# Tiles 0 and 1 on shared conv weight pieces, lent ring slots, casts in list order, six sgb buffers

## The chip, the cores and the metric

The kernel runs as one program on the eight cores of one Trainium2 chip; each core works on two of the sixteen sequences, with no exchange between cores. The metric is the device time in microseconds (us) of the slowest core. Engines are PE (TensorE), ACT (ScalarE), DVE (VectorE), POOL (GpSimd) and SP (SyncE); SP and POOL issue DMAs, and only POOL issues those that cast float32 to bfloat16.

## What is computed

One residual block (D_MODEL 1024, RG_W 1280, 16 heads of 80), from the reference:

```python
mod = silu(c) @ w_ada + b_ada; shift, scale, gate = split(mod, 3)
h = rmsnorm(x, g_norm) * (1 + scale) + shift
sc_b, sc_c, sc_v, sc_g, rg_v, rg_g, m_a, m_b = split(h @ w_in)     # 8704 columns
y_a = (sc_b * causal_conv3(sc_c * sc_v) * silu(sc_g)) @ sc_w_out
v = causal_conv4(rg_v)
r = sigmoid(v @ w_a + b_a); i = sigmoid(v @ w_x + b_x)             # block-diagonal
log_a = -8 * r * softplus(-lam)
y_rg[t] = exp(log_a) * y_rg[t-1] + sqrt(1 - exp(2 * log_a)) * i * v
y_b = (y_rg * silu(rg_g)) @ rg_w_out
merged = sigmoid(m_a + b0) * y_a + sigmoid(m_b + b1) * y_b
out = rmsnorm(x + gate * (merged @ w_out), g_final)
```

## The kernel before

A core's 4096 rows are eight tiles of 512 (NT = 8, tiles 0 to 3 are one sequence, 4 to 7 the other). Activations lie transposed, channels on partitions, so a product of 128 output channels is eight matmuls of 128x128 on 128x512 into one of seven PSUM banks. The work is a list of items (`program`, L243), each a letter with a tile and a number:

- P (L455): load 128 rows of x, Square with row sum on ACT, scale into xn (which lies in the four sgb buffers). T (L461): eight transposes of xn, two ACT evictions with scale and shift into hT.
- A, B (L494, L516): one of eight conv pieces, two products each (16 matmuls), output in pa. R (L533): one of ten RG-LRU channel blocks, two products; ACT copies into rbuf and vbuf and takes the tanh for the gate into sgb (L553), DVE does three taps (L555) and frees the gate's bank (L559). R uses vbuf and sgb number n % 4.
- G (L565): the block-diagonal gates of one block, 4 or 6 matmuls in all, from the resident weights wg; tanh and exp on ACT. After each odd block one pair of square roots (L602, L603) with a table load, then `g_tail` (L608) for both: product, scan, product with sgb into prg (L617).
- Z, Y (L619, L631): merge gates (16 matmuls) and the two down projections (8 and 10) of piece M; POOL adds into merged (L658). L, O (L664, L667): x rows again; output projection from resident wout (16 matmuls), gate, residual, norm, store.
- ADA, PRM, GATE (L740, L721, L766): the modulation from c. ADA uses four pieces at the start, GATE two, and writes gatebc, which O needs.

FIRST lists tile 0's A, R, G and tile 1's P, T. Then rounds of MIX: R, G of tile i between Z, Y of tile i - 1, then A, B of tile i between O of tile i - 1 and P, T of tile i + 1. LAST ends tile 7.

Weights stream through a ring of five slots of 1 MB (`ring`, NSLOT). The order of pieces is that of their first use. `pump` (L387) gives the next piece the next free slot: for tile 0 (and ada, gt) a cast DMA on POOL from float32, else a reload on SP from scratch wsc. At its first use a tile-0 piece is also stored to wsc on SP (`get`, L413; the DMA is issued at L418). `used` (L422) frees a slot after the piece's last item and pumps. wg is loaded ahead of piece A1, wout ahead of gt0, both with no wait since their buffers are their own.

The order of instructions on each engine is made by `Sched.schedule` (L97) from durations and dependences. PE keeps the list's order. Each other engine takes, among operations whose predecessors have been placed, the one with the earliest start and, among equals, the lowest index (L129). All engines then run in that order, SP and POOL too: a DMA that has to wait holds all that follow it on its queue.

Of the kernel before, what the change touches and what calls it, by code (L numbers as in the profile page):

```python
# [12 lines left out]
D = 1024  # L13
# [7 lines left out]
NSLOT = 5  # L21
PAD = 16
# [12 lines left out]
class Op:  # L35
    __slots__ = ("idx", "e", "fn", "raw", "order", "dur", "lat", "nbytes", "dsem", "pos", "fin")

    def __init__(self, idx, e, fn, dur, lat, nbytes, dsem):
        self.idx, self.e, self.fn, self.dur, self.lat, self.nbytes, self.dsem = idx, e, fn, dur, lat, nbytes, dsem
        self.raw, self.order = set(), set()  # L40
        self.pos = None
        self.fin = None


class Sched:
# [51 lines left out]
    def schedule(self):  # L97
# [9 lines left out]
        link = 0.0  # L107
# [8 lines left out]
        while done < n:  # L116
            best = None
            for e in ENGS:
# [6 lines left out]
                else:  # L125
# [3 lines left out]
                    cand = min((max(free[e], ready_at[i]), i, e) for i in lst)  # L129
# [87 lines left out]
def gate_pairs():  # L217
    pairs = []
    for j in range(NRC):
# [5 lines left out]
        for i in sorted(ins):  # L225
# [10 lines left out]
FIRST = ("R0 R1 A0 B0 R2 G0 R3 G1 A1 B1 R4 G2 A2 B2 R5 G3 A3 B3 R6 G4 R7 A4 B4 G5 R8 G6 R9 G7 A5 B5 G8 G9 P0 P1 P2 P3 "  # L236
         "A6 B6 T0 A7 T1 B7 T2 T3")
MIX = ("R0 R1 Z0 Y0 R2 Z1 G0 R3 Y1 G1 R4 Z2 G2 Y2 R5 Z3 G3 R6 Y3 G4 Z4 R7 G5 Y4 R8 Z5 G6 Y5 R9 Z6 G7 Y6 G8 Z7 G9 Y7 "
       "A0 B0 P0 P1 P2 L0 A1 B1 P3 L1 O0 A2 B2 L2 O1 A3 B3 L3 O2 A4 T0 B4 O3 A5 T1 B5 A6 T2 B6 A7 T3 B7")
# [3 lines left out]
def program():  # L243
# [4 lines left out]
    for i in range(NT + 1):  # L248
        text = FIRST if i == 0 else MIX if i < NT else LAST
        for word in text.split():  # L250
            k, j = word[0], int(word[1:])
            t = i - 1 if k in "ZYLO" else i + 1 if k in "PT" else i
            if t == NT:
                continue
            if i == 1 and word == "L0":
                p += [("GATE", 0), ("GATE", 1)]
            p.append((k, t, j))
# [3 lines left out]
def piece_of(it):  # L261
# [7 lines left out]
    if k in "AB":  # L269
        return ("A", it[1], it[2])  # L270
# [5 lines left out]
def build_nc():  # L276
# [30 lines left out]
    junk = sb([128, D], BF16, "junk"); junkB = S.buf("junk")  # L307
# [3 lines left out]
    pa = sb([128, 8, TT], BF16, "pa"); paB = [S.buf(f"pa{j}") for j in range(8)]  # L311
# [11 lines left out]
    merged = sb([128, 8, TT], BF16, "merged"); mergedB = [S.buf(f"mg{j}") for j in range(8)]  # L323
    ident = sb([128, 128], BF16, "ident"); identB = S.buf("ident")
    identf = junk[:].bitcast(F32)[:, 0:128]
    ones = junk[:].bitcast(F32)[:, 128:256]
# [49 lines left out]
    ring_state = {"next": 0, "free": list(range(NSLOT)), "where": {}}  # L376
# [10 lines left out]
    def pump():  # L387
        while ring_state["next"] < len(order) and ring_state["free"]:
            key = order[ring_state["next"]]
            slot = ring_state["free"].pop(0)  # L390
# [3 lines left out]
            dst = ring[slot][:, 0:nco]  # L394
            if key[0] in ("ada", "gt") or key[1] == 0:
# [59 lines left out]
    def it_P(i, s):  # L455
        xb, xbB = load_x(i, s)
        assert not any(o[1] < NRC and (o[0], o[1]) in gstate for o in owner.values())
        st, colB = rstd_of(xb[:], [xbB])
        dve(lambda e: e.tensor_scalar(out=xn[:, s, :], in0=xb[:], scalar1=st, scalar2=None, op0=ALU.mult), [xbB, colB], [xnB[s]], 0.75)

    def it_T(i, q):  # L461
# [3 lines left out]
        def tr(e):  # L465
            for kl in range(2):
                kc = 2 * q + kl
                for s in range(4):
                    ins = e.transpose(out=pst[:, kl, s * 128:(s + 1) * 128], in_=xn[:, s, kc * 128:(kc + 1) * 128], identity=ident[:])  # L469
            return ins  # L470
        S.op("pe", tr, reads=xnB + [identB], writes=[pstB], dur=1.0, lat=0.25)
# [22 lines left out]
    def it_A(i, j):  # L494
        key = ("A", i, j)
# [20 lines left out]
    def it_B(i, j):  # L516
        key = ("A", i, j)
# [8 lines left out]
        dve(lambda e: e.tensor_tensor(out=ub[:], in0=bb[:, :], in1=ub[:], op=ALU.mult), [bbB, ubB], [ubB])  # L526
        dve(lambda e: e.tensor_tensor(out=pa[:, j, :], in0=ub[:], in1=gb[:], op=ALU.mult), [ubB, gbB], [paB[j]])
# [5 lines left out]
    def it_R(i, j):  # L533
        key = ("R", i, j // 2)
# [7 lines left out]
        sg_, sgB_ = sgb[:, k, :], sgbB[k]  # L542
# [88 lines left out]
    def it_YM(i, j):  # L631
# [4 lines left out]
        w, wB = get(key)  # L636
        bya, byaB = nb()
# [15 lines left out]
        used(key)  # L653
        dve(lambda e: e.scalar_tensor_tensor(out=ga_[:], in0=ga_[:], scalar=1.0, in1=bya[:, :], op0=ALU.add, op1=ALU.mult),  # L654
# [247 lines left out]
```

How the kernel before makes its waits and increments, by code:

```python
            def body(engine):  # L171
                seen = {}
                def need(tokens):
                    want = {}
                    for sem, val in tokens:
                        if seen.get(sem, 0) < val and want.get(sem, 0) < val:
                            want[sem] = val
                    for sem, val in want.items():
                        seen[sem] = val
                        engine.wait_ge(sched.semobj[sem], val)
                for i in streams[e]:
                    o = ops[i]
                    need([ops[d].pos for d in sorted(o.raw)]
                         + [ops[d].pos for d in sorted(o.order) if e != "pe" or ops[d].e != e])
                    o.fn(engine).then_inc(sched.semobj[o.pos[0]], 16 if o.dsem is not None else 1)
                if e == "sp":
                    need([o.pos for o in last])
```

## Time and profile before

| | us |
|---|---|
| median of 3 runs | 1620.74 |
| lowest, highest | 1616.59, 1670.92 |
| the profiled execution | 1620.76 |
| its span on the slowest core (core 1) | 1619.2 |
| spans of the other cores | 1612.3 to 1618.9 |
| PE, DVE, ACT, POOL busy | 1437.8, 977.4, 882.9, 301.4 |

Busy times are sums over one core's span. Matmul records overlap a little, so a busy PE is not PE at its peak. Times of rows are us from the start of the span, on core 1; the granted clock is 1.00 at 2.4 GHz and 0.50 at 1.2 GHz.

### The profile page before, as it was taken

The numbers are of one execution on the slowest core, as the hardware profiler recorded it, in microseconds if no ns is written. First come the engines' busy times: TensorE is split into PE (matmuls) and PEld (weight loads), VectorE is DVE, ScalarE is ACT, GpSimd is POOL, SyncE is SP. The second block draws the span as 40 slices with busy tenths as digits, with TensorE's granted clock in tenths as the row PEclk, the third lists the DMA queues.
The fourth block names the chain that finished last, engine by engine and source line by source line (L and its number), as shares of the span: only waits on it lengthen the run. The fifth ranks groups of instructions, "written<-read, shape, count | busy, mean of one in ns | idle before, by whom it ended". The sixth has DMA issues, their size and how long they took to land.

```text
span 1619.2 us, 22766 instructions; the slowest of 8 cores (1612.3 to 1619.2 us)
## 1 busy us (share of the span) xinstructions
PE 1437.8 (89%) x6848; PEld 655.1 (40%) x6848; DVE 977.4 (60%) x1435; ACT 882.9 (55%) x1319; POOL 301.4 (19%) x534
## 2 busy tenths in 40 slices
PE   1049829899999999899999999999999999999996
PEld 1024314344444444344444444444444444444442
DVE  2027834577656775568656775568656775567614
ACT  3028835783567645774557645675466735774221
POOL 3002211321112211222111211222112210221011
PEclk9999969999999999999999999999999999999998
DMA  9999985888533563336533464336633474344621
GB/s 183 170 194 207 220 208 129 193 197 270 197 125 119 172 222 138 131 132 207 187 135 109 160 219 148 133 126 204 195 116 132 156 223 148 129 139 143 203 84 65
DMA packets 55688, 265.94 MB, mean 164 GB/s; under 512 B 4880, under 2 KB 6672, under 8 KB 34064
## 3 DMA queue, kind: packets, MB, share of 16 engines
q1 hardware_dynamic: 38592, 231.85, 42.6%
q0 software_dynamic: 16976, 32.64, 13.9%
q8 instruction: 58, 0.95, 0.2%
q14 instruction: 62, 0.51, 0.1%
HBM read 257.78 MB, written 39.32 MB: 183 GB/s over the span
## 4 chain that ended last, share of the span: by engine, by line
PE 83%; DMA 7%; ACT 3%; issue 2%; another core or an unknown queue 2%; DVE 1%; POOL 1%; SPq 0%; ACTq 0%; POOLq 0%; DVEq 0%
PE bank L487 57%; PE bank L650 8%; PE bank L680 7%; PE bank L642 6%; PE bank L582 5%; DMA ring_s<-wall 3%; DMA ring_s<-wm 2%; DMA xb_s<-x 2%; PE pst L469 1%; ACT ab_s L591 1%; DVE sgb_s L559 1%; ACT trb_s L587 1%; ACT gbuf_s L628 1%; ACT sgb_s L553 0%
## 5 line engine op out<-in xcount | busy, mean ns | idle before, releaser
L487 PE MATMUL bank<-hT_s,ring_s 128*128 128x512 bf16 x4352 | 980.8, 384 | 41.5 <-DVE sgb_s L559 37.7
L487 PEld LDWEIGHTS bank<-hT_s,ring_s 128*128 128x128 bf16 x4352 | 427.5, 99 | 565.4 <-issue 72.5
L555 DVE SCALAR_TENSOR_TENSOR vbuf_s<-rbuf_s,cst_s,vbuf_s 128x512 f32<-128x512 f32 x240 | 179.4, 748 | 129.9 <-ACT vbuf_s L551 121.4
L658 POOL TENSOR_TENSOR merged_s<-ubuf_s,gbuf_s 128x512 bf16<-128x512 f32 x64 | 85.7, 1339 | 366.8 <-DVE gbuf_s L656 366.7
L650 PE MATMUL bank<-prg_s,ring_s 128*128 128x512 bf16 x640 | 148.6, 379 | 0.0
L506 ACT ACTIVATE pbuf_s<-bank 128x512 f32<-128x512 f32 x64 | 38.0, 594 | 194.6 <-PE bank L487 177.5
L642 PE MATMUL bank<-pa_s,ring_s 128*128 128x512 bf16 x512 | 120.9, 379 | 0.0
L680 PE MATMUL bank<-wout_s,merged_s 128*128 128x512 bf16 x512 | 116.9, 383 | 2.5 <-POOL merged_s L658 2.5
L550 ACT ACTIVATE rbuf_s<-bank 128x512 f32<-128x512 f32 x80 | 47.5, 593 | 127.3 <-PE bank L487 126.1
L469 PE MATMUL pst<-ident_s,sgb_s 128*128 128x128 bf16 x256 | 21.5, 233 | 105.0 <-ACT hT_s L474 68.4
L596 DVE SCALAR_TENSOR_TENSOR tib_s<-tib_s,vbuf_s 128x512 f32<-128x512 f32 x80 | 61.9, 780 | 72.6 <-ACT tib_s L589 72.6
L582 PE MATMUL bank<-vb_s,wg_s 128*128 128x512 bf16 x416 | 102.7, 379 | 0.0
L616 POOL COPY hst_s<-trb_s 128x1 f32<-128x1 f32 x80 | 78.4, 982 | 121.6 <-DVE trb_s L614 117.0
L614 DVE TENSOR_TENSOR_SCAN trb_s<-ab_s,hst_s,tib_s 128x512 f32<-128x512 f32 x80 | 98.0, 1265 | 0.0
L450 ACT ACTIVATE junk_s<-xb_s 128x1024 bf16<-128x1024 f32 x32 | 33.8, 1056 | 112.2 <-DMA xb_s<-x 106.9
L650 PEld LDWEIGHTS bank<-prg_s,ring_s 128*128 128x128 bf16 x640 | 62.6, 98 | 75.5
L654 DVE SCALAR_TENSOR_TENSOR ubuf_s<-ubuf_s,bank 128x512 f32<-128x512 f32 x64 | 43.7, 683 | 80.9 <-PE bank L642 80.8
L626 ACT ACTIVATE ubuf_s<-bank,prm_s 128x512 f32<-128x512 f32 x64 | 43.9, 686 | 70.0 <-PE bank L487 69.8
L508 DVE TENSOR_TENSOR pbuf_s<-bank,pbuf_s 128x512 f32<-128x512 f32 x64 | 44.1, 689 | 58.7 <-PE bank L487 57.0
L559 DVE SCALAR_TENSOR_TENSOR sgb_s<-sgb_s,bank 128x512 f32<-128x512 f32 x80 | 54.6, 683 | 37.8 <-ACT sgb_s L553 37.6
L680 PEld LDWEIGHTS bank<-wout_s,merged_s 128*128 128x128 bf16 x512 | 50.4, 99 | 64.4 <-issue 5.1
L642 PEld LDWEIGHTS bank<-pa_s,ring_s 128*128 128x128 bf16 x512 | 50.1, 98 | 60.4
(86 smaller groups left out, 1564.9 us busy)
## 6 DMA issues: line engine op xcount, KB each, us to landing
ring_s<-wsc SPq DMA_DIRECT2D x91, 1024.0 KB, 5.7
ring_s<-wsc SPq DMA_DIRECT2D x56, 1088.0 KB, 5.5
xb_s<-x SPq DMA_DIRECT2D x64, 512.0 KB, 5.0
out<-vbuf_s SPq DMA_DIRECT2D x32, 512.0 KB, 4.3
ring_s<-wall POOLq DMA_DIRECT2D x13, 1024.0 KB, 32.9
wsc<-ring_s SPq DMA_DIRECT2D x13, 1024.0 KB, 11.3
ring_s<-wm POOLq DMA_DIRECT2D x8, 1088.0 KB, 13.9
wsc<-ring_s SPq DMA_DIRECT2D x8, 1088.0 KB, 8.9
```

The source lines that it names most:

```text
L487: ins = e.matmul(bk[:, :], lhsT=w[:, o:o + 128], rhs=hT[h][:, kc, :], start=(kc == 0), stop=(kc == 7))
L550: act(lambda e: e.activation(out=rb_[:, 3:3 + TT], in_=brv[:, :], func=AF.Copy), [brvB], [rbB_], 0, True)
L555: dve((lambda e, t=t, w=w: e.scalar_tensor_tensor(out=v_, in0=rb_[:, t:t + TT], scalar=w, in1=v_, op0=ALU.mult, op1=ALU.add)), [rbB_, vB_, ...
L559: dve(lambda e: e.scalar_tensor_tensor(out=sg_, in0=sg_, scalar=1.0, in1=brg[:, :], op0=ALU.add, op1=ALU.mult), [sgB_, brgB], [sgB_])
L582: ins = e.matmul(bk[:, :], lhsT=wg[:, g, gi, :], rhs=rhs_l[t][:], start=(t == 0), stop=(t == len(prs) - 1))
L596: dve(lambda e: e.scalar_tensor_tensor(out=ti_[:], in0=ti_[:], scalar=1.0, in1=v_, op0=ALU.add, op1=ALU.mult), [tiB_, vB_], [tiB_])
L614: dve(lambda e: e.tensor_tensor_scan(out=tr_[:], data0=a_[:], data1=ti_[:], initial=hst[:, j:j + 1], op0=ALU.mult, op1=ALU.add), [aB_, tiB ...
L616: pool(lambda e: e.tensor_copy(out=hst[:, j:j + 1], in_=tr_[:, TT - 1:TT]), [trB_], [hstB[j]])
L642: ins = e.matmul(bya[:, :], lhsT=w[:, o:o + 128], rhs=pa[:, kc, :], start=(kc == 0), stop=(kc == 7))
L650: ins = e.matmul(byb[:, :], lhsT=w[:, o:o + 128], rhs=prg[:, h, kc, :], start=(kc == 0), stop=(kc == NRC - 1))
L658: pool(lambda e: e.tensor_tensor(out=merged[:, j, :], in0=ga_[:], in1=gb_[:], op=ALU.add), [gaB_, gbB_], [mergedB[j]], 1.27)
L680: ins = e.matmul(bk[:, :], lhsT=merged[:, kc, s * 128:(s + 1) * 128], rhs=wout[:, kc, hh * 512:(hh + 1) * 512], start=(kc == 0), stop=(kc ...
```

## The change

1. **Shared A pieces.** `piece_of` gives A and B items of tiles 0 and 1 the same piece, so each conv piece is loaded once for both tiles. R pieces of tile 1 are still reloaded. FIRST and the first MIX become three parts, H0, H1 and H2; lower case r, g, a, b are items of tile 1, V is GATE. Tile 1's conv output goes to `pa_1`, in ring slot 4, which joins the ring after Y7 of tile 1; its xn goes to merged.
2. **Lent slots.** Slots 5 and 6 are the two halves of wout, 7 is gatebc; A pieces 0 to 4 may use 5, 6 and 0 to 3, tile 0's R pieces 7 and 0 to 3, all others 0 to 4.
3. **Late residents.** wg is loaded ahead of R piece 2, wout ahead of M piece 0, waiting for slots 5 and 6.
4. **Scheduler.** Every operation gets a due time: for PE the sum of durations before it, for others that plus SLACK or what its users need. Among equal starts the earlier due goes first. Casts on POOL go in list order. The link's model has its own rate for casts and shares it with SP's transfers. Durations and latencies are set anew.
5. **sgb has six buffers** and R uses n % 6. junk is gone: Square writes its result into xn or the x buffer, and the start's identity and ones lie in vbuf.
6. **Rounds from tile 2 on** are MIXR (the old first half) and MIXA, with T items about one A, B pair earlier.

```diff
@@ schedule
+        t = 0.0
+        for o in ops:
+            if o.e == "pe":
+                o.due = t
+                t += o.dur
+            else:
+                o.due = t + SLACK
+        for o in reversed(ops):
+            for d in o.raw | o.order:
+                p = ops[d]
+                if p.e != "pe":
+                    p.due = min(p.due, o.due - p.dur - p.lat)
...
-                    cand = min((max(free[e], ready_at[i]), i, e) for i in lst)
+                    lst = [i for i in lst if e != "pool" or not ops[i].nbytes or i == casts[cast_next]]
+                    if not lst:
+                        continue
+                    cand = min((max(free[e], ready_at[i]), ops[i].due, e, i) for i in lst)
+                    cand = (cand[0], cand[3], e)
...
+            if o.nbytes and e == "pool":
+                cast_next += 1
+                link["pool"] = max(link["pool"], start + 1.0) + o.nbytes / 292e3
+                o.fin = link["pool"] + o.lat
...
-FIRST = ("R0 R1 A0 B0 R2 G0 R3 G1 A1 B1 R4 G2 A2 B2 R5 G3 A3 B3 R6 G4 R7 A4 B4 G5 R8 G6 R9 G7 A5 B5 G8 G9 P0 P1 P2 P3 "
-         "A6 B6 T0 A7 T1 B7 T2 T3")
...
+H0 = ("A0 B0 R0 R1 P0 P1 P2 P3 A1 B1 T0 R2 T1 G0 T2 R3 T3 G1 a0 b0 R4 G2 a1 b1 R5 G3 A2 B2 R6 G4 a2 b2 R7 G5 A3 B3 R8 G6 a3 b3 R9 G7 "
+      "A4 B4 r0 G8 a4 b4 r1 G9")
+H1 = "A5 B5 r2 g0 a5 b5 r3 g1 V0 A6 B6 r4 g2 a6 b6 r5 g3 V1 A7 B7 r6 g4 a7 b7 r7 g5 Z0 r8 g6 Z1 r9 g7 Y0 g8 Z2 g9"
+H2 = "Y1 P0 Z3 Y2 P1 Z4 Y3 P2 Z5 Y4 P3 Z6 Y5 Z7 Y6 T0 Y7 T1 T2 L0 L1 O0 T3 L2 O1 L3 O2 O3"
+MIXR = ("R0 R1 Z0 Y0 R2 Z1 G0 R3 Y1 G1 R4 Z2 G2 Y2 R5 Z3 G3 R6 Y3 G4 Z4 R7 G5 Y4 R8 Z5 G6 Y5 R9 Z6 G7 Y6 G8 Z7 G9 Y7")
+MIXA = "A0 B0 P0 P1 P2 L0 A1 B1 P3 L1 O0 A2 B2 L2 O1 A3 T0 B3 L3 O2 A4 B4 T1 O3 A5 B5 T2 A6 B6 T3 A7 B7"
...
-        return ("A", it[1], it[2])
+        return ("A", it[1] if it[1] > 1 else 0, it[2])
...
+    pa_1 = ring[NSLOT - 1][:, 0:8 * TT].rearrange("p (k t) -> p k t", k=8); paB_1 = [S.buf(f"pb{j}") for j in range(8)]
...
+    NSG = 6
+    sgb = sb([128, NSG, TT], F32, "sgb"); sgbB = [S.buf(f"sgb{k}") for k in range(NSG)]
...
+    MM = 0.213
+    T_PS = {0: 0.5, 1: 0.59, 2: 0.88}
+    T_SB = {0: 0.53, 1: 0.63, 2: 0.9}
...
+    wflat = wout[:].rearrange("p k n -> p (k n)")
+    slots += [wflat[:, 0:4096], wflat[:, 4096:8192], gatebc[:].rearrange("p b n -> p (b n)").bitcast(BF16)]
...
+    ring_state = {"next": 0, "free": [0, 1, 2, 3, 5, 6, 7], "where": {}}
...
-            slot = ring_state["free"].pop(0)
+            lend = (5, 6, 0, 1, 2, 3) if key[0] == "A" and key[1] == 0 and key[2] < 5 else (7, 0, 1, 2, 3) if key[0:2] == ("R", 0) else range(NSLOT)
+            fit = [k for k in ring_state["free"] if k in lend]
+            if not fit:
+                break
+            slot = min(fit, key=lend.index)
...
-        sg_, sgB_ = sgb[:, k, :], sgbB[k]
+        sg_, sgB_ = sgb[:, n % NSG, :], sgbB[n % NSG]
...
+        if i == 1 and j == 7:
+            ring_state["free"].append(NSLOT - 1)
+            pump()
...
-    before_piece[("A", 0, 1)] = [lambda: S.dma("pool", lambda e: e.dma_start(
+    before_piece[("R", 0, 2)] = [lambda: S.dma("pool", lambda e: e.dma_start(
...
-    before_piece[("gt", 0)] = [lambda: S.dma("pool", lambda e: e.dma_start(out=wout[:], in_=wout_d[:, :, 0:1024]), writes=[woutB],
+    before_piece[("M", 0, 0)] = [lambda: S.dma("pool", lambda e: e.dma_start(out=wout[:], in_=wout_d[:, :, 0:1024]), writes=[woutB] + lentB[0:2],
```

## Rows read from the trace of the kernel before

**Rows 1.** Busy time by stages, core 1; first line: the columns

```profile
core 1: us, PE busy (x) PEld busy (x) DVE busy (x) ACT busy (x) POOL busy (x), PEclk, DMA share, GB/s
0.00:45.00 45.00, 6.84 (x152) 6.15 (x152) 11.85 (x61) 13.96 (x23) 13.35 (x26) 1.00 0.97 181
45.00:100.00 55.00, 0.04 (x1) 0.07 (x2) 0.15 (x1) 1.82 (x3) 0.44 (x1) 1.00 1.07 182
100.00:182.00 82.00, 80.11 (x366) 36.14 (x367) 58.58 (x86) 60.16 (x89) 18.87 (x41) 1.00 1.02 200
182.00:251.00 69.00, 30.77 (x144) 13.59 (x142) 33.54 (x51) 37.50 (x55) 11.49 (x20) 0.72 0.84 208
251.00:439.80 188.80, 184.03 (x869) 83.92 (x870) 123.27 (x174) 109.58 (x164) 40.20 (x70) 0.99 0.77 200
439.80:1530.30 1090.50, 1061.69 (x4986) 482.22 (x4984) 721.61 (x1025) 644.34 (x962) 202.83 (x365) 0.99 0.47 158
```

**Rows 2.** Chain of waits, start-up and first rounds: start us, us, what

```profile
382.77 3.45 PE bank L680 x16
...
410.40 0.45 PE pst L469 x8
...
436.36 13.81 PE bank L487 x64
```

**Rows 3.** Timeline, PE, 0 to 105 us: start, us, line, xcount, idle before

```profile
99.96 1.01 PE L469 MATMUL pst<-ident_s,sgb_s 128*128 128x128 bf16 x8 [56.43 <-ACT hT_s L474]
...
102.86 2.72 PE L487 MATMUL bank<-hT_s,ring_s 128*128 128x512 bf16 x6 [1.89 <-ACT hT_s L474]
```

**Rows 4.** Timeline, ACT, 0 to 105 us

```profile
98.00 1.06 ACT L450 ACTIVATE junk_s<-xb_s 128x1024 bf16<-128x1024 f32 x1 [55.87 <-DMA xb_s<-x]
```

**Rows 5.** Timeline, SP's DMA queue: issues, 48 to 218 us

```profile
48.82 0.33 SPq L418 DMA_DIRECT2D wsc<-ring_s  x1
...
83.52 0.33 SPq L418 DMA_DIRECT2D wsc<-ring_s  x1
...
84.04 0.47 SPq L444 DMA_DIRECT2D xb_s<-x  x1
...
204.28 0.32 SPq L418 DMA_DIRECT2D wsc<-ring_s  x1
...
217.41 0.32 SPq L418 DMA_DIRECT2D wsc<-ring_s  x1
```

**Rows 6.** Timeline, POOL: DMA issues, 6 to 8 us

```profile
6.10 1.13 POOL L794 DMA_DIRECT2D wg_s<-wg  x1
...
7.22 0.96 POOL L797 DMA_DIRECT2D wout_s<-wout  x1
```

**Rows 7.** Timeline, PE, 180 to 240 us

```profile
187.43 9.50 PE L487 MATMUL bank<-hT_s,ring_s 128*128 128x512 bf16 x32 [4.22 <-DVE sgb_s L559]
...
236.48 1.01 PE L469 MATMUL pst<-ident_s,sgb_s 128*128 128x128 bf16 x8 [30.30 <-DVE stat_s L451]
```

**Rows 8.** DMA queues and one kind of issue, from the page

```profile
q1 hardware_dynamic: 38592, 231.85, 42.6%
q0 software_dynamic: 16976, 32.64, 13.9%
ring_s<-wsc SPq DMA_DIRECT2D x91, 1024.0 KB, 5.7
```

**Rows 9.** Waits, 439.8 to 1530.3 us: us in total, times, longest

```profile
PE bank L487 <- DVE sgb_s L559: 28.8, 12, 2.8
```

**Rows 10.** Timeline, ACT, 650 to 664 us

```profile
654.65 1.28 ACT L602 ACT_TABLE_LOAD   x1
...
663.26 0.58 ACT L553 ACTIVATE sgb_s<-bank 128x512 f32<-128x512 f32 x1
```

**Rows 11.** Timeline, DVE, 659 to 665 us

```profile
660.97 1.27 DVE L617 TENSOR_TENSOR prg_s<-trb_s,sgb_s 128x512 bf16<-128x512 f32 x2
```

**Rows 12.** Timeline, PE, 676 to 700 us

```profile
687.59 5.15 PE L487 MATMUL bank<-hT_s,ring_s 128*128 128x512 bf16 x16 [2.79 <-DVE sgb_s L559]
```

More of the change, by code:

```diff
@@ L21 @@
 NSLOT = 5
+SLACK = 30.0
 PAD = 16
@@ L247, in program, with add @@
     p += [("PRM",)]
-    for i in range(NT + 1):
-        text = FIRST if i == 0 else MIX if i < NT else LAST
+    def add(text, i, im, ip):
         for word in text.split():
             k, j = word[0], int(word[1:])
-            t = i - 1 if k in "ZYLO" else i + 1 if k in "PT" else i
-            if t == NT:
+            if k == "V":
+                p.append(("GATE", j))
                 continue
-            if i == 1 and word == "L0":
-                p += [("GATE", 0), ("GATE", 1)]
-            p.append((k, t, j))
+            t = im if k in "ZYLO" else ip if k in "PT" else 1 if k in "rgab" else i
+            if t < NT:
+                p.append((k.upper(), t, j))
+    add(H0, 0, 0, 1)
+    add(H1, 0, 0, 1)
+    add(H2, 0, 0, 2)
+    for i in range(2, NT):
+        add(MIXR, i, i - 1, i + 1)
+        add(MIXA, i, i - 1, i + 1)
+    add(LAST, NT, NT - 1, NT)
     return p
@@ L323, in build_nc, with xn_of @@
     merged = sb([128, 8, TT], BF16, "merged"); mergedB = [S.buf(f"mg{j}") for j in range(8)]
+    xn1 = merged[:].rearrange("p k t -> p (k t)").rearrange("p (s d) -> p s d", s=4)
+    def xn_of(i):
+        return (xn1, [mergedB[2 * s:2 * s + 2] for s in range(4)]) if i == 1 else (xn, [[sgbB[s]] for s in range(4)])
     ident = sb([128, 128], BF16, "ident"); identB = S.buf("ident")
-    identf = junk[:].bitcast(F32)[:, 0:128]
-    ones = junk[:].bitcast(F32)[:, 128:256]
+    identf = vbuf[:, 0, 0:128]
+    ones = vbuf[:, 0, 128:256]
+    junkB = vbufB[0]
     mhalf = sb([128, 1], F32, "mhalf"); constB = S.buf("const")
@@ L375, in build_nc @@
             uses[key] += 1
-    ring_state = {"next": 0, "free": list(range(NSLOT)), "where": {}}
+    slots = [r[:] for r in ring]
+    slotB = [[b] for b in ringB]
+    slotB[NSLOT - 1] += paB_1
+    wflat = wout[:].rearrange("p k n -> p (k n)")
+    slots += [wflat[:, 0:4096], wflat[:, 4096:8192], gatebc[:].rearrange("p b n -> p (b n)").bitcast(BF16)]
+    lentB = [S.buf(f"lent{k}") for k in range(3)]
+    slotB += [[b] for b in lentB]
+    ring_state = {"next": 0, "free": [0, 1, 2, 3, 5, 6, 7], "where": {}}
     wscB = [S.buf(f"wsc{p}") for p in range(NPIECE)]
@@ L393, in pump @@
             nco = ncols(key)
-            dst = ring[slot][:, 0:nco]
+            dst = slots[slot][:, 0:nco]
             if key[0] in ("ada", "gt") or key[1] == 0:
@@ L468, in tr @@
                 for s in range(4):
-                    ins = e.transpose(out=pst[:, kl, s * 128:(s + 1) * 128], in_=xn[:, s, kc * 128:(kc + 1) * 128], identity=ident[:])
+                    ins = e.transpose(out=pst[:, kl, s * 128:(s + 1) * 128], in_=xn_[:, s, kc * 128:(kc + 1) * 128], identity=ident[:])
             return ins
-        S.op("pe", tr, reads=xnB + [identB], writes=[pstB], dur=1.0, lat=0.25)
+        xn_, xnB = xn_of(i)
+        S.op("pe", tr, reads=[b for s in range(4) for b in xnB[s]] + [identB], writes=[pstB], dur=0.9, lat=0.25)
         for kl in range(2):
```

64 lines of the change are left out of this document (33 added, 31 removed).

## The prediction

> **What bounds the kernel now.** I read the table by stages first [rows 1]: for each stretch it gives the busy time of every engine, the granted clock and the DMA share. What TensorE (PE) misses is not spread evenly: it works 6.8 us of the first 45, nothing to 100, 30.8 of the 69 from 182 to 251, and then nearly all. From 439.8 to 1530.3 (six rounds, tiles 2 to 7) it works 1061.7 of 1090.5. So there are two losses: a start of 440 us in which the weights come in, and a small one that repeats.
>
> The prices of PE come from the chain [rows 2]: 64 matmuls take 13.81 us, so 0.2158 each and 3.45 for an item of 16; the eight transposes of one T item take 0.45. The list from tile 0 to the end of the first mixed round holds 936 matmuls of A, B, R, G for two tiles, 336 of Z, Y, O and 32 of GATE, 1304 in all or 281.4 us, and 12 T items, 5.4 us. The last B of that round ends at 439.8 (the piece of 13.81 us from 436.36 is B7 and the first three items of tile 2). Some 150 us of it are idle.
>
> The first hole: PE's fourth T item starts at 99.96, after 56.4 us of nothing, and the first conv or RG product at 102.86 [rows 3]. It waited for an eviction by ScalarE (ACT), which itself stood 55.9 us in front of a Square for tile 1, until 98.00 [rows 4]. Its x load was issued at 84.04, since SP stood before two stores of pieces to scratch, which had to wait until the pieces had landed, at 48.82 and 83.52 [rows 5]. The second piece was late because POOL had issued the gate weights (6.10) and the output weights (7.22) ahead of it [rows 6], though the output weights are first read at 382.8 [rows 2]. The second hole is the same: PE goes dry at 206, and its T item waits until 236.48 [rows 7] for x loads that stood behind the store at 217.41 [rows 5].
>
> The DMA engines are full in that time (share 0.97 to 1.07 up to 182 and still 0.84 to 251, [rows 1]), so they are a bound by themselves. Their prices: the casting queue moved 32.64 MB in 13.9% of the span, 145 GB/s, so a 1.05 MB piece takes 7.2 us, gate weights 11.8, output weights 14.5; the other queue moved 231.85 MB in 42.6%, so a store or reload takes 3.1 us, an x load 1.6 [rows 8]. Cross-check: from the store at 83.52 to that at 204.28 eleven pieces landed [rows 5], 11.0 us for a piece with its store and a bit of x and reload, against 7.2 + 3.1 = 10.3.
>
> The repeating loss: in the six middle tiles PE waits 28.8 us, in 12 waits, for one thing, the vector instruction of L559 that frees an RG gate bank, and this is the whole idle time [rows 9]. In one such case the tanh of L553 comes only at 663.26, while L617, which releases the sgb of four channels earlier, ran at 660.97 [rows 10, 11]; in between ACT did what it had been given instead. A round of 804 matmuls and four T items needs 175.3 us; six need 1050 (the last has no T). 1090.5 were taken: 40.5 too many, 28.8 of waits and about 12 at low clock behind them.
>
> **The change, part by part.** *Shared A pieces.* Tile 1 no longer reloads eight conv pieces: 8 x 3.1 = 25 us of DMA gone in a saturated stretch, and each cast piece now feeds 13.8 us of PE and not 6.9.
>
> *Order of casts, late output weights.* Walking through the new list with the prices above (casts in list order, stores, x loads and reloads added when they can start, slots as the list frees them): four ada pieces by 44, A0 lands and PE starts at 51.5 instead of 102.9. The next items wait: R0 3.4, A1 3.4, R2 2.9, and G0 10.9 for the gate weights, at 97.2. From there each conv piece feeds two tiles and PE runs without waiting. V0 ends at 221.9, 124.7 us of PE later; it frees the slot for A7, which lands at 237.8 behind gt1. Then DMA is the bound again: output weights 14.4, eight M pieces of 7.65 (61.2), eight stores (26), three x loads and a reload (8) bring M7 in at about 349. Behind it stand Z7, Y6, Y7, four T and four O items, 26.8 us: the first three list parts end at 376.5. The same by sum: 51.5 + 285 of PE work + 20.6 waits before G0 + 19.4 waits in Z. Against 439.8 this is 63 earlier.
>
> *What the walk leaves out.* One tile's A, R and G with its T and P items took, from 100 to 251, PE 110.9 us, ACT 97.7 and VectorE (DVE) 92.1 [rows 1]. PE at full clock needs about 103, so ACT would be 95% full and DVE 89%, now for 200 us on end and with in-order queues. I allow 8 us of PE waits (bounds: 0, since PE ran 80 of 82 us in the first part of that; and 20, three times the wait of 4.22 at 183 to 187 with its low clock, 9.50 us for what takes 6.91 at full, [rows 7]). Gain 55. With casts at 6.8 us (the stretch 48.82 to 83.52 gives 4.85 MB in 31.6, [rows 5]) the walk ends at 370, with 7.6 at 385.
>
> *Six sgb buffers.* The tanh waits for the channel six back, whose release lies over 20 us earlier. Both waits of each tile should go with their low clock. I take 28.5 of the 40.5 us: 2 us a tile stay, since ACT's sqrt pair with its table loads of 1.28 still stands between tanh and bank [rows 10]. Bounds: 0 and 40.
>
> *Order by PE's need, new durations, T items earlier.* No instruction is added. They decide who is first on ACT, DVE and SP; bank evictions ahead of work for later buffers. Nothing of its own in the sum; worth -10 to +15 by how they fill the 40.5. The Square now writes into the x buffer or xn instead of junk, so an x buffer is held about 2 us longer; three buffers cover that. Casts in fixed order can hold POOL in front of halo copies and the merge; PE's one kind of wait in the rounds is another [rows 9].
>
> *Lent slots.* Slot 4 holds tile 1's conv output until Y7 of tile 1, so the first round of tile 2 has four slots. Each is freed over 10 us ahead of its use and a reload lands in 5.7 [rows 8]: nothing.
>
> Sum: 1619.2 - 55 - 28.5 = 1535.7 us. The profiled execution took 1620.76 with what lies round the span, the median of the runs shown is 1620.74: 1.5 more, so 1537 us.
>
> **Rivals.** (a) *The repeating wait moves, it doesn't go.* trb, tib and ab stay at three and vbuf at four; G5 needs what the sqrt pair of G3 frees. For it: ACT runs 107 us a round [rows 1], over half of it in the R part. Against it: no PE wait of these tiles is put down to them [rows 9]. Only the start gains: 1565.
> (b) *The start stalls again on x.* SP still runs in order, x loads of tile 2 lie among the M stores, which land 11 us apart; the last T items then wait for M7 at 349 plus load and normalisation, 10 to 20 us. In tile 1 there is cover: its T0 comes at 80, its loads are issued by 35. 1537 + 15: about 1552 to 1570 with some of (a).
> (c) *PE starts cold.* Between the first pieces PE idles. After the wait at 684.8 to 687.6 sixteen matmuls took 5.15 us and not 3.45 [rows 12], so a gap costs clock; after the hole of 56 us the first six took 2.72 [rows 3]. If all 24 us of work before G0 ran at half clock (1.2 GHz), it would take 48 of the 45.7 us there are: 2 to 4 us late, 1541. The Trainium skill, "TensorE: Matmul & The Clock Gate", section "HAM oscillation", says that a matmul stream which waits for DMA between pieces starts each piece at the low clock again; the rows on low clock agree. By that rule sharing pieces would bring less in the starved part.
> (d) *The other side, slower.* The new order feeds bank evictions first and the recurrence later, so the R and Z parts stall more in every tile. The start's 55 us are used up if each of six tiles waits 9.2 us more than today's 6.7, that is some four or five waits like today's two with their clock loss; at 14.6 more it would be 2% slower (1653). For it: a list order only guessed from durations set the two present waits. Against it: DVE is 66% and ACT 59% busy in these rounds [rows 1].
> (e) *Sharing does nothing*: only order mattered. Then 25 us of DMA come back in the start: 1555 to 1560.
>
> **Chances.** Forecast with (c) 0.55; (a) 0.15; (b) 0.13; (e) 0.08; (d) 0.04; something better, all waits gone and casts at 6.8 (1513 to 1520), 0.05. The time is that of the likeliest. Bounds of the main case: 1619.2 - 70 - 36 = 1513 to 1619.2 - 42 - 15 = 1562; the range goes on to 1578 to take in (a), (b) and (e), and leaves (d) out. About 2%, 32 us, is what a measurement of this kernel tells from no change. Faster by more than that (under 1588) gets 0.91: all but (d) are 0.96, less 0.05 for tails of (a), (b) and (e) where two of them meet. Within 2%: those 0.05 and 0.01 of (d), 0.06. Slower 0.03, the rest of (d).
>
> **What would show it.** First product of bank L487 near 52; wait on the gate weights near 97; output weights issued after 190; end of the third list part near 385; PE waits for Z items on DMA of 3 to 5 us each; in the middle tiles about 177 us per tile and no wait on L559. It is wrong if PE still has a hole of over 20 us before 250, if casts take 8 us a piece beside stores (then the start ends at 393 plus waits, gain 38), or if the tiles stay at 182.

## The result and the profile after

The changed kernel takes 1574.7 us (four executions, 1573.3 to 1582.1) against 1623.2 us for the kernel before on the same chip: ratio 0.9724, interval 0.9673 to 0.9774. It is faster by 48.5 us; 83.7 were forecast, and the range ended at 1578.

Line numbers moved: L542 is the old L487 (products of A, B, R, Z), L638 a G product, L523 a transpose, L609 the RG tanh, L615 the vector instruction that frees the RG gate bank (old L559), L607 the eviction into vbuf, L707 and L740 the Y and O products, L718 the addition into merged, L497 a load of x, L749 and L751 the last vector instruction and the store of an O item.

Spans and granted clock of each core, profiled execution of the changed kernel:

```profile
core 0: 1547.1 us, clock 0.983
core 1: 1538.6 us, clock 0.983
core 2: 1570.2 us, clock 0.966
core 3: 1571.7 us, clock 0.966
core 4: 1540.6 us, clock 0.986
core 5: 1549.6 us, clock 0.983
core 6: 1548.0 us, clock 0.983
core 7: 1538.7 us, clock 0.987
```

Six cores end at 1538.6 to 1549.6, core 1 within 3 us of the forecast span of 1535.7. Cores 2 and 3 end over 20 us later, at a lower mean clock, and the slowest core is the time. So there are two accounts to read: core 1 against the prediction's steps, and core 3 against core 1. In some executions of either kernel a pair of cores or a whole die runs at a lower clock than the others, so below figures are compared within one chip and, where it matters, on cores that kept full clock.

Busy time by stages, core 1, the columns as in [rows 1]; the last line is the stretch from the first product to the end of the first three list parts:

```profile
45.00:117.00 72.00, 45.09 (x231) 20.70 (x232) 22.52 (x38) 29.91 (x46) 6.16 (x17) 0.88 1.06 208
117.00:310.00 193.00, 192.00 (x890) 86.72 (x888) 155.14 (x226) 148.45 (x217) 40.83 (x90) 1.00 0.82 177
310.00:391.30 81.30, 63.97 (x291) 28.12 (x290) 30.36 (x40) 25.85 (x37) 16.06 (x18) 0.90 0.85 213
391.30:1452.00 1060.70, 1054.88 (x4994) 482.37 (x4993) 733.45 (x1037) 652.98 (x972) 185.90 (x370) 1.00 0.49 165
...
56.66:391.30 334.64, 299.06 (x1369) 133.81 (x1370) 206.65 (x295) 200.84 (x293) 61.33 (x123) 0.95 0.87 191
```

The two holes of [rows 1] are gone: from 117 to 310 PE misses 1.0 us of 193. The first three list parts end at 391.3 (before 439.8). What is left is 17.3 us of idle PE from 310 to 391 and 5.8 in the rounds. (The rounds end at 1450.1, so they take 1059 us; the fourth line runs 2 us further.)

Timeline of PE in the start, core 1, answering [rows 3]:

```profile
56.66 8.76 PE L542 MATMUL bank<-hT_s,wout_s 128*128 128x512 bf16 x32 [7.84 <-DMA wout_s<-wall]
...
75.23 7.07 PE L542 MATMUL bank<-hT_s,wout_s 128*128 128x512 bf16 x32 [1.36 <-DMA wout_s<-wall]
...
86.14 5.30 PE L542 MATMUL bank<-hT_s,ring_s 128*128 128x512 bf16 x16 [3.39 <-DMA ring_s<-wall]
...
102.01 1.86 PE L638 MATMUL bank<-vb_s,wg_s 128*128 128x512 bf16 x4 [10.13 <-DMA wg_s<-wg]
...
227.37 3.62 PE L840 MATMUL bank<-ring_s,gfin_s 128*128 128x512 bf16 x16
...
344.73 6.33 PE L542 MATMUL bank<-hT_s,ring_s 128*128 128x512 bf16 x16 [5.37 <-DMA ring_s<-wm]
...
360.96 5.05 PE L542 MATMUL bank<-hT_s,ring_s 128*128 128x512 bf16 x16 [6.02 <-DMA ring_s<-wm]
```

Waits of PE on core 1, from 45 to 400, the three largest (us in total, times, longest):

```profile
PE bank L542 <- DMA ring_s<-wm: 15.9, 5, 6.0
PE bank L638 <- DMA wg_s<-wg: 10.1, 1, 10.1
PE bank L542 <- DMA wout_s<-wall: 9.2, 2, 7.8
```

and from 390 to 1540, all of them, answering [rows 9]:

```profile
PE bank L707 <- ACT vbuf_s L607: 5.8, 1, 5.8
PE bank L740 <- POOL merged_s L718: 2.5, 1, 2.5
```

The twelve waits on the gate bank are gone. One new wait stands there, on vbuf, once in the kernel. The one on merged_s comes behind the last round, outside the stretch of [rows 9], and the kernel before has it too, at the same 2.5 us.

Core 3 in the stretch in which it falls behind, and below it pieces of the same work, first at core 3's low level, then on core 3 after it, then on core 1 (48 products in one run without a pause):

```profile
116.00:272.00 156.00, 156.00 (x596) 64.64 (x595) 107.56 (x156) 99.21 (x143) 21.16 (x63) 0.81 0.65 137
```
```profile
143.05 12.78 PE L542 MATMUL bank<-hT_s,ring_s 128*128 128x512 bf16 x48
...
288.07 10.52 PE L542 MATMUL bank<-hT_s,ring_s 128*128 128x512 bf16 x48
```
```profile
147.08 10.52 PE L542 MATMUL bank<-hT_s,ring_s 128*128 128x512 bf16 x48
```

PE is busy for all 156 us, waits for nothing, and its granted clock is 0.81, neither of the two levels in the rows of before. Dividing each row by its 48 matmuls, one costs 0.266 us there and 0.219 outside. The trace has the level from 113.2 to 273.9, 160.7 us, so it costs 160.7 x 0.19 = 30 us; core 3 ends its first three list parts at 425.9, core 1 at 391.3, and both take the same six rounds (1057 and 1059).

### The profile page after: what moved, and what is told of

It is laid out like the page before. It is cut to its first block, busy times and chain, and to the rows that moved or that the text cites. A ratio compares the mean times of both kernels' runs of the same rounds, so it can differ in the third digit from the quotient of the medians.

```text
span 1571.7 us, 22758 instructions; the slowest of 8 cores (1538.6 to 1571.7 us)
## 1 busy us (share of the span) xinstructions
PE 1460.2 (93%) x6848; PEld 661.4 (42%) x6848; DVE 982.3 (62%) x1435; ACT 888.7 (57%) x1319; POOL 270.5 (17%) x534
## 3 DMA queue, kind: packets, MB, share of 16 engines
q0 software_dynamic: 16976, 32.64, 14.6%
## 4 chain that ended last, share of the span: by engine, by line
PE 88%; DMA 7%; another core or an unknown queue 1%; DVE 1%; issue 1%; ACT 1%; POOL 0%; POOLq 0%; DVEq 0%; ACTq 0%; SPq 0%
PE bank L542 60%; PE bank L707 8%; PE bank L740 7%; PE bank L699 6%; PE bank L638 6%; DMA ring_s<-wm 4%; DMA xb_s<-x 1%; DMA ring_s<-wada 1%; PE pst L523 1%; DMA out<-vbuf_s 1%; PE bank L840 0%; POOL stat_s L505 0%; DVE vbuf_s L749 0%; ACT hT_s L529 0%
## 5 line engine op out<-in xcount | busy, mean ns | idle before, releaser
L542 PE MATMUL bank<-hT_s,ring_s 128*128 128x512 bf16 x4096 | 929.1, 386 | 20.3 <-DMA ring_s<-wm 20.3
L542 PEld LDWEIGHTS bank<-hT_s,ring_s 128*128 128x128 bf16 x4096 | 405.3, 99 | 519.1 <-issue 89.2
L707 PE MATMUL bank<-prg_s,ring_s 128*128 128x512 bf16 x640 | 150.4, 382 | 5.2 <-ACT vbuf_s L607 5.2
L718 POOL TENSOR_TENSOR merged_s<-ubuf_s,gbuf_s 128x512 bf16<-128x512 f32 x64 | 86.8, 1356 | 328.2 <-DVE gbuf_s L716 311.0
L607 ACT ACTIVATE vbuf_s<-bank,cst_s 128x512 f32<-128x512 f32 x80 | 62.0, 776 | 100.5 <-PE bank L542 95.2
L638 PE MATMUL bank<-vb_s,wg_s 128*128 128x512 bf16 x416 | 106.6, 390 | 11.8 <-DMA wg_s<-wg 11.3
L740 PE MATMUL bank<-wout_s,merged_s 128*128 128x512 bf16 x512 | 114.9, 379 | 2.5 <-POOL merged_s L718 2.5
L670 DVE TENSOR_TENSOR_SCAN trb_s<-ab_s,hst_s,tib_s 128x512 f32<-128x512 f32 x80 | 107.4, 1350 | 0.0
L699 PE MATMUL bank<-pa_s,ring_s 128*128 128x512 bf16 x448 | 105.8, 379 | 0.0
L707 PEld LDWEIGHTS bank<-prg_s,ring_s 128*128 128x128 bf16 x640 | 63.0, 98 | 82.2 <-issue 7.9
L669 DVE TENSOR_TENSOR tib_s<-tib_s,trb_s 128x512 f32<-128x512 f32 x80 | 63.6, 836 | 35.0 <-ACT trb_s L659 34.9
L565 ACT ACTIVATE ubuf_s<-pbuf_s,prm_s 128x512 f32<-128x512 f32 x64 | 51.8, 809 | 50.0 <-DVE pbuf_s L563 40.8
L613 ACT ACTIVATE vb_s<-vbuf_s 128x512 bf16<-128x512 f32 x80 | 50.2, 628 | 46.4 <-DVE vbuf_s L611 45.1
L529 ACT ACTIVATE hT_s<-pst,prm_s 128x512 bf16<-128x512 bf16 x64 | 49.6, 775 | 46.9 <-PE pst L523 41.8
L740 PEld LDWEIGHTS bank<-wout_s,merged_s 128*128 128x128 bf16 x512 | 49.7, 98 | 61.4 <-issue 2.9
L716 DVE SCALAR_TENSOR_TENSOR gbuf_s<-gbuf_s,bank 128x512 f32<-128x512 f32 x64 | 43.9, 685 | 43.9 <-PE bank L707 43.9
```

What stands on the lines that cost most here:

```text
L542: ins = e.matmul(bk[:, :], lhsT=w[:, o:o + 128], rhs=hT[h][:, kc, :], start=(kc == 0), stop=(kc == 7))
L565: act(lambda e: e.activation(out=ub[:], in_=pb[:, 2:2 + TT], func=AF.Identity, scale=w2, bias=bia), [pbB, prmB], [ubB], 2)
L607: act(lambda e: e.activation(out=v_, in_=brv[:, :], func=AF.Identity, scale=w3, bias=bia), [brvB, cstB], [vB_], 2, True)
L638: ins = e.matmul(bk[:, :], lhsT=wg[:, g, gi, :], rhs=rhs_l[t][:], start=(t == 0), stop=(t == len(prs) - 1))
L669: dve(lambda e: e.tensor_tensor(out=ti_[:], in0=ti_[:], in1=tr_[:], op=ALU.mult), [tiB_, trB_], [tiB_])
L670: dve(lambda e: e.tensor_tensor_scan(out=tr_[:], data0=a_[:], data1=ti_[:], initial=hst[:, j:j + 1], op0=ALU.mult, op1=ALU.add), [aB_, tiB ...
```

## Experiments

Every kernel ran on eight cores. Chips A to D are four chips, and on each the kernel before was measured too. Chip A: before 1626.2. The changed kernel itself did not run on chip A; where it is needed beside the runs of chip A, its figures are those of chip C, 1550 to 1552 us with all cores at full clock, the kernel before taking 1621.8 there.

**Six sgb buffers taken back.**

```diff
-    NSG = 6
+    NSG = 4
```

> The changed kernel with four sgb buffers. Theory: the wait on the gate bank comes back in rounds 2 to 7, two per round, 28.8 us of waits and 12 us at low clock in the kernel before; the rounds take 1059 us on core 1 now and would take about 1090, the cores with full clock about 1539 + 30 = 1570, the slowest 1600. Rival: the order by due time would have removed the wait without the buffers; then nothing changes, 1574.

Measured: 1598.2 us, ratio 0.9831 (0.9816 to 0.9847), no core at 0.81 in the profile. So 47 us are lost against 1550 to 1552, or 43 when each is set against the kernel before on its own chip. On core 1 the six rounds take 1101.4 us, 42.5 more, and the old wait is back, in its old number:

```profile
PE bank L542 <- DVE sgb_s L615: 29.9, 12, 4.0
```

So with this order the buffers are worth all of the surplus that [rows 9] and its low clock made up, not the 28.5 us of the forecast. The rounds are even 11 us longer than before the change (1090.5); a wait of 5.2 us on vbuf, of which more below, is in them too.

**Sharing undone**, six buffers and the new scheduler kept. The lent slots and the new lists go back with it, so that T items come as late as before, and wg is loaded ahead of R piece 1; the run can't tell these parts from sharing itself.

```diff
-H0, H1, H2, MIXR, MIXA (shared lists)
+FIRST, MIX (lists of before)
-        return ("A", it[1] if it[1] > 1 else 0, it[2])
+        return ("A", it[1], it[2])
-            lend = (5, 6, 0, 1, 2, 3) if ... else range(NSLOT)
+            lend = range(NSLOT)
-    ring_state = {"free": [0, 1, 2, 3, 5, 6, 7], ...
+    ring_state = {"free": [0, 1, 2, 3, 4], ...
```

> The old lists FIRST and MIX, a ring of five slots, A pieces of tile 1 reloaded, nothing lent; with the new scheduler (casts in list order, output weights late, due times, durations) and six sgb buffers. Theory: sharing is worth the DMA of eight reloads, 25 us, and twice the PE work per piece at the start. By a walk of the old list PE starts with R0 near 52 and then waits for pieces that come every 10.5 us and feed 6.9: the A, R, G part of tile 0 (111 us of PE) ends near 52 + 13 x 10.5 + 12 + 10 = 211 instead of 182 to 206 before, so the start ends 25 to 40 us later than in the changed kernel: cores at full clock 1565 to 1580. Rival, only the order mattered: 1540 to 1550 on such cores. If the drop to 0.81 hangs on PE being dense while DMA is full, this one has less of it.

Measured: 1568.6 us, ratio 0.9644 (0.9627 to 0.9661), no core at 0.81 in the profile. Sharing with its lists and slots is worth 13 to 17 us (the former with each kernel set against the kernel before on its own chip). On core 1 the first product comes at 57.96, about as early as with sharing (56.66), and the start ends at 419.5. So the order of the casts and the late residents give the first 20 us, sharing 28 more. But the rounds run without any wait, from 419.5 to 1470:

```profile
419.50:1470.00 1050.50, 1050.50 (x4984) 480.50 (x4985) 726.05 (x1028) 646.82 (x968) 187.21 (x368) 1.00 0.48 164
```

That is the ideal of the prediction (1050), where the changed kernel takes 1059. The new lists give 8 us back in the first round. Why is seen in the changed kernel: VectorE writes the results of O2 and O3 of tile 0 into vbuf (first fence), SP issues the store of O2's at 401.10, within 0.1 us of the end of that write (second), and ACT's evictions for R0 and R1 of tile 2 into the same buffers (third) wait until 408.42, with PE behind ACT:

```profile
399.75 1.28 DVE L749 SCALAR_TENSOR_TENSOR vbuf_s<-vbuf_s,stat_s,gfin_s 128x1024 f32<-128x1024 f32 x1
...
401.90 1.28 DVE L749 SCALAR_TENSOR_TENSOR vbuf_s<-vbuf_s,stat_s,gfin_s 128x1024 f32<-128x1024 f32 x1 [0.81 <-POOL stat_s L505]
```
```profile
400.28 0.33 SPq L497 DMA_DIRECT2D xb_s<-x  x1
401.10 2.50 SPq L751 DMA_DIRECT2D out<-vbuf_s  x2
```
```profile
408.42 1.45 ACT L607 ACTIVATE vbuf_s<-bank,cst_s 128x512 f32<-128x512 f32 x2 [5.84 <-DMA out<-vbuf_s]
```

SP's queue did not hold the store back: the x load ahead of it was issued at 400.28, before the results were there. The list left no room: H2 ends with O2 and O3, and R0 of tile 2 follows at once, while in MIX and MIXA six A and B items stand between O3 and the next R, and there the wait doesn't come. That is read from lists and rows; no run moved these items alone.

**Is it data that pulls the clock down?** Tiles 0 and 1 with their hT rows set to zero. The eviction into hT becomes a Copy with scale 0 in place of an Identity with scale and shift; every other instruction is left.

```diff
+            if i < 2:
+                act(... e.activation(out=hT[h][:, kc, :], in_=pst[:, kl, :], func=AF.Copy, scale=0.0) ...)
+                continue
```

> The changed kernel with hT written as zeros for tiles 0 and 1 (so the output rows of these two tiles are not the reference's; every instruction, size and wait is the same, only the moving data of the first 390 us are zero). In the changed kernel two of eight cores ran 160 us at a granted clock of 0.81, from about 115 to 272 us, and lost 30 us; the other six ended at 1539 to 1550. Theory 1, the low clock answers to the electrical load of the dense start: with zeros it stays away, all cores at 1.00 there, spans of 1539 to 1550, time about 1548. Theory 2, it answers to how busy PE is, or comes by itself: some cores still show 160 us at 0.81, time 1573 to 1582.

Measured: 1555.3 us, ratio 0.9568 (0.9551 to 0.9585), and no 0.81 in its profile.

**Or the idle gap ahead of the dense stretch?** 48 more matmuls ahead of G0, in the 10 us in which PE waits for the gate weights.

```diff
+            if (i, j, g) == (0, 0, 0):
+                def dummy(e, bk=bk):   # 48 matmuls of hT[0] into G0's bank
```

> The changed kernel with 48 extra matmuls of 512 columns on tile 0's data in front of G0, where PE stands 10 to 12 us for the gate weights. Their results are overwritten. They need 10.4 us at full clock and fill the gap. Theory 1a, what brings 0.81 is the step of load when eight cores start together after a gap: no gap, no 0.81 at 115 us, time about 1548. Theory 1b, it is the level of the load with all engines and DMA busy: 0.81 comes as before or earlier, by up to 10 us, on as many cores or more; time 1573 to 1590.

Measured: 1552.1 us, ratio 0.9541 (0.9519 to 0.9563). The gap is filled, core 1:

```profile
93.43 10.52 PE L638 MATMUL bank<-hT_s 128*128 128x512 bf16 x48
103.79 1.03 PE L644 MATMUL bank<-vb_s,wg_s 128*128 128x512 bf16 x4
```

Both theories could claim this pair of runs, since nothing shows that the unchanged kernel would have met the level on chip A. So it ran beside the warmed one on chip B. In one further execution of the warmed kernel the pair of cores 6 and 7 showed 0.967 (1579 us), which already spoke against the gap.

**Chip B**: before 1682.3. The same kernel again, warmed again, the order and scheduler alone (sharing undone and NSG = 4), and due times switched off:

```diff
-cand = min((max(free[e], ready_at[i]), ops[i].due, e, i) for i in lst)
+cand = min((max(free[e], ready_at[i]), 0, e, i) for i in lst)
```

> The changed kernel itself, unchanged, beside its variants and the kernel before on one chip. In its first measurement every execution had two to five cores with 160 us at a granted clock of 0.81, and 1573 to 1582 us; the variants with zero data and with the gap filled, measured on another chip, had none and took 1552 to 1555. Theory 1, the drop belongs to this kernel's start (gap, then all engines at once): it comes again, 1573 to 1582 us. Theory 2, it belongs to the chip it ran on: no drop here, 1548 to 1556 us, as e2_warm_gap.

> The kernel of e2_warm_gap (48 extra matmuls fill PE's wait for the gate weights) on the same chip as e5_changed_again. If the gap is the cause, this one takes about 1550 and e5 about 1574. If the cause is the chip, both agree within 3 us.

> The kernel of e4_no_share with four sgb buffers: of the change only the scheduler (casts in list order, due times, durations) and the late output weights are left, with the old lists. e4_no_share took 1568 and the kernel before 1626 on one chip. Theory: six buffers are worth about 45 us in the rounds (e3_sgb4 against the changed kernel), so this one takes about 1568 + 45 = 1613, and order alone gives 10 to 20 us. Rival: order alone gives most of the 58 us, 1580, and the buffers little without sharing.

> The changed kernel, but among operations that can start at the same time the scheduler takes the one listed first, as before, and not the one due first. Casts stay in list order, durations and buffers as changed. Theory (the prediction gave this part nothing of its own, between -10 and +15 us): within 10 us of the changed kernel on the same chip. Rival: due times are what empties the rounds of waits; then the rounds take 1080 to 1100 us instead of 1059 and the time rises by 20 to 40 us.

Measured: changed 1609.1, warmed 1611.7, order alone 1661.9, index order 1645.6. On this chip every execution of every kernel had cores below full clock; in the profiles the 0.81 level comes on all cores, in stretches of up to 19 us. Changed and warmed agree within 3 us: the gap theory fell. Order alone gains 20.5 of the 73 us. Index order was thought small and costs 36.5. The medians hold the low level too, so the rounds are read on the cores that met it least: core 4, with one stretch of 15 us at 0.81 in its rounds, waits (first fence, index order) where the changed kernel (second, the same core, also one stretch) does not:

```profile
PE bank L542 <- DVE sgb_s L615: 22.7, 6, 4.1
PE bank L707 <- ACT vbuf_s L607: 5.2, 1, 5.2
```
```profile
PE bank L707 <- ACT vbuf_s L607: 5.7, 1, 5.7
PE bank L740 <- POOL merged_s L718: 2.5, 1, 2.5
```

The rounds of cores 4 to 7 take 1092 to 1097 us with index order, against 1060 and 1061 on cores 4 and 5 of the changed kernel. With six buffers and no due times six of the twelve waits are still there, 22.7 of the 28.8 us; with due times and four buffers all twelve are. In order alone the start ends at 416 on cores 6 and 7, and their rounds take 1120 us, ten stretches of 15 us at 0.81 among them; without these, by an estimate from 150 us x 0.19, about 1092, no less than before the change. Both are needed.

**Chip C**: before 1621.8. The changed kernel a third time, and a version meant to be better: the output weights cast ahead of A piece 6, not of M piece 0, since on core 1 of the changed kernel the DMA share from 190 to 200 is 0.01 and PE later waits for M pieces.

```diff
-    before_piece[("M", 0, 0)] = [... wout ...
+    before_piece[("A", 0, 6)] = [... wout ...
```

> The changed kernel once more beside the kernel before. On the first chip each execution had cores with one stretch of 160 us at a granted clock of 0.81 (1574 us, ratio 0.972); on the chip of e5 both kernels had many short ones (1609 against 1682, ratio 0.957). Theory: the drop is the chip's answer, not this kernel's: on a chip that keeps 1.00 the kernel before takes 1620 to 1626 and this one 1548 to 1556, ratio 0.953 to 0.957, all cores within 15 us of each other. Rival: it belongs to this kernel's start and shows on such a chip too, 1573 to 1582, ratio 0.972.

> The changed kernel with one move: the output weights are loaded ahead of conv piece 6, not ahead of M piece 0. Their slots 5 and 6 are free at about 195 us, when the DMA engines stand nearly idle (share 0.01 from 190 to 200 in the changed kernel, since the ring is full), and from 230 to 390 DMA is the bound. Theory: 14.5 us of casting move out of the bound stretch; the waits of Z items, 16 to 22 us, fall by 10 to 14 us and the time by as much: 10 to 14 below e9. Rival: conv piece 6 now lands 14 us later and PE waits there instead, no gain.

Measured: the changed kernel 1560.3, ratio 0.9593 (0.9541 to 0.9645), in two groups: 1550.0, 1551.4 and 1551.9 with all cores at full clock, and 1568.7, 1572.0 and 1576.4 with one to three pairs of cores at a mean of 0.964 to 0.967. In the profiled one the pair is 6 and 7, and the low level lies elsewhere in the kernel, on core 6 from 371 to 533 with a break of 3 us; most of the second part:

```profile
436.00:531.00 95.00, 94.38 (x356) 39.38 (x362) 57.03 (x76) 66.27 (x95) 18.03 (x30) 0.81 0.36 126
```

So neither expectation held whole: the level came on a chip on which the kernel before kept its clock, but it is not bound to the start.

Output weights sooner: ratio 0.9524 (0.949 to 0.9557); the two executions at full clock took 1542.6 and 1547.5, 3 to 9 us under the changed kernel's. But the mechanism that was expected did not occur: POOL issues the output weights at 200 to 206 in place of 231 to 234, and PE's waits for M pieces stay as they were, 16.0 to 20.9 us on the eight cores against 14.6 to 21.9, and so does the end of the start, 390 to 399 against 390 to 400. The M pieces are cast at the same times as before, on core 1 the first at 255 against 254 and the last at 332 against 336, since POOL issues each when a slot comes free. With two executions against three, and the intervals of the ratios overlapping, a gain is not shown.

**Chip D**: before 1672.0. The changed kernel, and the same with hT zero in all tiles (`i < 2` above becomes `i < 99`).

> The changed kernel beside e11 and the kernel before. Theory: executions with all cores at full clock take 1550 to 1552, those with a pair or more at 0.81 for 160 us take 1568 to 1582; the share of the latter is well above that of the kernel before on the same chip (4 of 4 against 1 of 4 on the first chip, 3 of 6 against 2 of 11 on that of e9). Rival: the share is that of the kernel before, and the first chip's four were chance.

> The changed kernel with hT written as zeros for all eight tiles (so all output rows differ from the reference's; instructions, sizes and waits are the same, the moving data of all conv, RG and merge-gate products are zero). On the chip of e9 three of six executions of the changed kernel had a pair of cores at 0.81 for 160 us (1569 to 1576 against 1550 to 1552). Theory 1, the drop answers to electrical load: with zeros it never comes, every execution 1550 to 1553, while e12 beside it shows it in some. Theory 2, it answers to activity or to nothing in the kernel: it comes as often as in e12.

Measured: changed 1587.0, and all eight of its executions had cores below full clock; zero rows 1551.9, and in all six executions (1548.8 to 1553.3) all cores read 0.980 or more. Core 0 from 533 to 547, changed kernel first, zero rows second:

```profile
533.00:547.00 14.00, 13.91 (x55) 5.81 (x54) 10.47 (x15) 3.00 (x5) 1.54 (x4) 0.82 0.63 197
```
```profile
533.00:547.00 14.00, 13.89 (x70) 6.62 (x71) 11.95 (x18) 4.87 (x9) 2.36 (x4) 1.00 0.68 229
```

PE is busy for the same 13.9 us and does 55 matmuls in the one and 70 in the other. So with the same list, waits and gaps the kernel loses 35 us on this chip or nothing. What differs is the data, and ACT's eviction into hT, 0.594 us in place of 0.775, on which PE does not wait in the rounds. Neither a wait nor a gap of the program alone is the cause; the data is a condition.

## Why the prediction was right and wrong

**The account.** 1571.7 - 1535.7 = 36.0 us over the forecast span. Core 1 is 2.9 of it. The slowest of the cores at full clock ends 11.0 after core 1, and core 3 another 22.1 after that: the level cost core 3 some 30 us, and without it core 3 would have ended among the others.

**The step that failed** is the price of a matmul, 0.2158 us for every product behind the start. It was taken from rows at full clock [rows 2], with half clock behind gaps [rows 12] as the only other level. A third level, 0.81, was no term, and rows 1 to 12 have none. Where the stretch of 160.7 us comes it costs 20 to 30 us on the slowest core, and all four executions of the result had it on at least one pair, the three without a trace by their mean clocks (0.957 to 0.968). Without it the changed kernel took 1550 to 1552 on chip C and 1549 to 1553 with zero rows on chip D: inside the range, 14 over the forecast.

**The spread of cores** was no term either. Core 1 was the slowest before, at 1619.2, with the others down to 1612.3; it is the fastest after. The cores at full clock end their start at 391 to 403 (before, 434 to 443), and then take the same rounds (1057 to 1060). Core 5, the last, waits 22.9 us for M pieces and 13.5 for those in wout's slots, core 1 15.9 and 9.2. The time is the slowest of eight, and here that is 11 us later than the account of core 1.

**The start: mechanism right, size near.** Forecast and core 1: first product 51.5 and 56.7, G0 97.2 and 102.0 with a wait of 10.9 and 10.1, V0's end 221.9 and 230.8, end 384.5 and 391.3. The gain is 48.5, not 55; core for core it is 35 to 48 on the six at full clock. The output weights are issued at 232.3. The 8 us allowed for ACT and DVE did not occur (1.0 us idle from 117 to 310, though ACT was busy 77% and DVE 80%), and the walk itself was 15 short: the first piece came 5 late, and from there PE was busy 299.1 us where 285 were reckoned and idle 35.6 where 40 were. Of the 14 us of work too many some 12 are matmuls at half clock behind waits; the walk priced them all at full. Waits for M pieces summed to 15.4 in four, against 19.4.

**The rounds: sum right, parts wrong.** Forecast 28.5 gained, measured 31.5 (1090.5 to 1059). But the buffers with the order take all 40, and the new lists give 8 back. "Order by PE's need: nothing of its own" holds for the order with four buffers, not in the sum: without due times 32 to 37 us of the 40 come back, so bounds of -10 to +15 were too narrow. "Lent slots: nothing" held, no reload is waited for in the rounds. What was not looked at is the seam of the new lists, where R0 of tile 2 needs a vbuf that O2 of tile 0 has just filled.

**Luck.** That core 1 came within 3 us of its forecast is in part luck: 15 us too few in the walk stand against 8 that were allowed and not needed, and 8 us at the seam against 12 more from the buffers than were counted.

**The rivals.** (a) fell: no repeating wait moved to trb, tib, ab or vbuf; the one on vbuf comes once. (b) fell: PE had no wait behind a late x load. (c), PE cold, held and was priced too low. 32 products took 8.76 us behind a wait of 7.84, and 16 took 5.30, 6.33 and 5.05 behind 3.39, 5.37 and 6.02, where full clock gives 7.07 and 3.62 (rows at 75.23 and 227.37). It was priced at 2 to 4 up to G0 and at nothing behind it; up to the end of the start it comes to 12. (d) fell. (e) fell: without sharing the start ends 28 us later, near the 25 of the prediction. The rule of the Trainium skill, "TensorE: Matmul & The Clock Gate", section "HAM oscillation", that a DMA-paced matmul stream starts its pieces at the low clock, agrees with these rows; the pieces behind waits of 1.39 and 1.36 us ran at full clock. Filling the one gap at G0 with matmuls did not make the kernel faster by more than 3 us.

**What stays open.** Why one pair of cores is taken and when. The changed kernel and its sooner variant had a pair at a mean clock of 0.964 to 0.969 in 7 of 12 executions on chip C, the kernel before in none of 11. On chip A the kernel before had such a pair in one of 9, and the three variants with full data in one of 12; on chips B and D every execution of both kernels had pairs below 0.97. So a kernel that keeps PE denser may meet it more often, or the counts may be chance: only the data was varied alone. Open too is why the start ends later on one core than on another.

## What to carry to other kernels

Add up a forecast for each core and take the slowest: a start bound by DMA spreads the cores, and one stretch at a lower clock on two of them can take back a third of the gain. More buffers and the order in which engines take work are one term, not two: neither removed the wait here without the other. When a list is cut anew, look at its seams: the last results of one tile and the first evictions of the next can need one buffer with no work between them. And before a load is moved to where the DMA engines idle, ask what the later ones wait for; here it was a free slot.

## What the runs showed of the hardware

Besides 1.00 and 0.50 the granted clock took a level of 0.81 while PE was busy without a pause: 48 matmuls in 12.78 us against 10.52. In every kept trace it held for both cores of a pair (0 and 1, 2 and 3, 4 and 5, 6 and 7). In the profiled execution of the result it came as one stretch of 160.7 us, on chip C as two of 48 and 111 us (core 6). On chip D it came as fourteen stretches of 15 us on each core of one die and as eleven or twelve of 4 to 6 us on each of the other, on chip B (changed kernel) as over forty of 4 to 19 us on each core of one die and as four to eleven of 15 us on each of the other. With zeroed rows it came in none of six executions on a chip where eight of eight had it. In some executions of either kernel all four cores of a die had a mean clock of 0.81 to 0.83, such as cores 4 to 7 of the changed kernel on chip D (0.813 to 0.815, 1834.1 us) and of the kernel before on chip A (0.818 to 0.823, 1881.8 us); no trace of one was kept. The Trainium skill, "TensorE: Matmul & The Clock Gate", Part 1, knows a limit of 13/16 of the clock that takes a whole die once three of its cores run dense matmuls, holds while the load lasts, and spares zeroed operands. The level, the zero rows and the executions with a whole die at it agree. In the others all eight cores ran dense, on chips A and C for over 1000 us at 1.00, and the level came by pairs and went while PE stayed busy; in that the runs differ, and they decide.
